# RG-LRU gates of a hybrid decoder trunk: one 64-row product per head for both gates, input gates moved between partitions by DMA

## What is computed

```python
def rg_lru(u, w_a, b_a, w_x, b_x, lam):
    ub = u.reshape(bsz, seq, N_RNN_BLOCKS, RNN_BLOCK)          # 16 heads of 64
    r = sigmoid(einsum('bsnc,ncd->bsnd', ub, w_a) + b_a)       # recurrence gate
    i_gate = sigmoid(einsum('bsnc,ncd->bsnd', ub, w_x) + b_x)  # input gate
    log_a = -8.0 * r * softplus(-lam)
    a = exp(log_a)
    beta = sqrt(-expm1(2.0 * log_a))
    b = beta * (i_gate * u)
    # h_t = a_t * h_{t-1} + b_t
```

## Time and profile before

| | us |
|---|---|
| median of 3 runs (1827.29 to 1829.1) | 1828.26 |
| the profiled execution, its own time | 1829.26 |
| its span, first to last instruction | 1827.6 |
| TensorE busy / weight loads | 1784.1 / 1564.4 |
| VectorE busy | 1488.7 |
| ScalarE busy | 1303.0 |
| POOL busy | 107.7 |
| gate products (L1923), 64 records | 15.6 |

### The profile page before, as it was taken

One profiled execution on the slowest core, in us unless ns is written; L12 is line 12 of the kernel. 1 busy time (PEld: TensorE's weight loads), 2 busy tenths in 40 slices (PEclk: granted clock), 3 DMA queues, 4 the chain that ended last, 5 costly groups with the idle time before them and its releaser, 6 DMA issues.

```text
span 1827.6 us, 29753 instructions
## 1 busy us (share of the span) xinstructions
PE 1784.1 (98%) x10521; PEld 1564.4 (86%) x10521; DVE 1488.7 (81%) x1948; ACT 1303.0 (71%) x1726; POOL 107.7 (6%) x138
## 2 busy tenths in 40 slices
PE   6999999999999999999999999999999999999997
PEld 6998999999879999978888888888888888888785
DVE  7888667666468886669989989989899898998996
ACT  6756547454477657567888888788888888888786
POOL 1200000000010200012000000010000000000300
PEclk8999999999999999999999999999999999999999
DMA  9663565565545744667999999999999999999991
GB/s 308 205 191 117 177 201 187 185 200 201 192 153 174 221 149 141 202 190 260 395 384 387 375 380 387 370 388 382 369 388 374 382 383 374 383 376 382 393 363 48
DMA packets 276048, 517.01 MB, mean 283 GB/s; under 512 B 10754, under 2 KB 114052, under 8 KB 275972
## 3 DMA queue, kind: packets, MB, share of 16 engines
q1 hardware_dynamic: 268400, 493.81, 76.3%
q0 software_dynamic: 7248, 22.06, 3.7%
q10 hardware_dynamic: 324, 0.12, 0.0%
HBM read 503.87 MB, written 7.88 MB: 280 GB/s over the span
## 4 chain that ended last, share of the span: by engine, by line
PE 84%; DVE 8%; ACT 6%; issue 2%; DMA 1%; DVEq 0%; SPq 0%; ACTq 0%
PE bank L1768 79%; DVE wlo L1115 3%; ACT whi L656 1%; PE bank L2225 1%; DMA raw<-in_moe_w_gate_dram 1%; ACT SC L832 1%; PE bank L1923 1%; ACT SQJ L667 1%; DVE RIN L1222 1%; DVE SC L1250 1%; ACT SC L827 0%; PE bank L1879 0%; ACT HH L714 0%; PE bank L2235 0%; DVE HL L1133 0%
## 5 line engine op out<-in xcount | busy, mean ns | idle before, releaser
L1115 DVE TENSOR_TENSOR wlo<-raw,whi 128x1024 fp32r<-128x1024 f32 x880 | 1030.1, 1221 | 154.8 <-ACT whi L656 151.8
L656 ACT ACTIVATE whi<-raw 128x1024 fp32r<-128x1024 f32 x880 | 919.9, 1059 | 308.7 <-PE bank L1768 300.9
L1768 PE MATMUL bank<-HH,whi 128*128 128x256 f32 x1296 | 364.0, 281 | 0.0
L1768 PE MATMUL bank<-HL,whi 128*128 128x256 f32 x1296 | 360.1, 278 | 0.0
L1768 PE MATMUL bank<-HH,wlo 128*128 128x256 f32 x1296 | 360.1, 278 | 0.0
L1768 PE MATMUL bank<-whi,XGH 128*128 128x512 f32 x896 | 355.0, 396 | 1.8 <-DVE wlo L1115 1.6
L1768 PE MATMUL bank<-whi,XGL 128*128 128x512 f32 x896 | 350.4, 391 | 0.0
L1768 PE MATMUL bank<-wlo,XGH 128*128 128x512 f32 x896 | 349.4, 390 | 0.0
L1768 PEld LDWEIGHTS bank<-HH,whi 128*128 128x128 f32 x1296 | 243.8, 188 | 0.9 <-issue 0.7
L1768 PEld LDWEIGHTS bank<-HH,wlo 128*128 128x128 f32 x1296 | 244.5, 189 | 0.0
L1768 PEld LDWEIGHTS bank<-HL,whi 128*128 128x128 f32 x1296 | 243.8, 188 | 0.2
(11 more groups left out here) (349 smaller groups left out, 2073.0 us busy)
## 6 DMA issues: line engine op xcount, KB each, us to landing
raw<-in_moe_w_gate_dram SPq DMA_DIRECT2D x112, 1024.0 KB, 7.2
raw<-in_moe_w_up_dram SPq DMA_DIRECT2D x112, 1024.0 KB, 7.7
raw<-in_moe_w_down_dram SPq DMA_DIRECT2D x112, 1024.0 KB, 6.0
raw<-in_w_in_dram SPq DMA_DIRECT2D x56, 1024.0 KB, 6.0
raw<-in_ffn_w_gate_dram SPq DMA_DIRECT2D x14, 1024.0 KB, 5.0
raw<-in_ffn_w_up_dram SPq DMA_DIRECT2D x14, 1024.0 KB, 5.0
raw<-in_ffn_w_down_dram SPq DMA_DIRECT2D x14, 1024.0 KB, 5.0
raw<-in_w_proj_a_dram SPq DMA_DIRECT2D x8, 1024.0 KB, 5.3
```

Source lines behind the costliest of these rows:

```text
L656: nc.scalar.activation(whi[b % SPL][:, r], raw[b % RAW][:, r], ACT.Copy).then_inc(s_hi, 1)
L1115: v.tensor_tensor(wlo[b % SPL][:, r], raw[b % RAW][:, r], whi[b % SPL][:, r].bitcast(F32), ALU.subtract).then_inc(s_lo, 1)
L1768: ins = mm(dst, a, b, start=start and n == 0, stop=stop and n == 2, skip_group_check=True)
```

## The change

- BD becomes half as large: for tile t, rows of head h hold both its matrices side by side, the recurrence gate's in columns 64h to 64h+63 and the input gate's in the other 64. No zeros are needed, and both memsets go.
- A gate product is one product of 64 rows per head: the head's 64 rows of BD and of U. Its 128 output rows are the head's recurrence gates on the head's own partitions and its input gates on the other half. The two heads go to two banks, (3, 7) or (5, 6).
- So Sigmoid of head 0 goes to T2 and that of head 1 to IG: each of the two tiles holds recurrence gates on one half of the partitions and input gates on the other. Tanh and Exp need the recurrence gates alone, so each is issued twice, over 64 partitions. The wait (`link`) moves behind the second Sigmoid.
- The input gates go to their own partitions in a new tile IX by DMA, issued by POOL within `exchange`, two transfers of 64 partitions for each pair of tiles (`input_halves`), when ScalarE has written the pair (`s_gx`). `input_gates` multiplies IX by U and waits for all 8 transfers of the layer (`s_ix`), as do the decays.
- IX lies where V goes, so the copies of V wait for `recurrence_input`.
- The two biases are loaded in four pieces in the order of the new output rows; 9 loads in place of 7.

```diff
         o_bd = o_rin + 8 * KB + LANE
-        BD = at("BD", o_bd, [P, 2, KT, P])
+        BD = at("BD", o_bd, [P, KT, P])
...
         V = at("V", o_q + 16 * KB, [P, BLK, D])
+        IX = at("IX", o_q + 16 * KB, [P, KT, SEQ])
...
+        LRU_BANK = ((3, 7), (5, 6))
...
-                        pool.dma_start(BD[HD * h:HD * h + HD, kind, :, HD * h:HD * h + HD], pairs[h]).then_inc(s_bd, 16)
-
-            pool.wait_ge(s_bdz, 1)
+                        d = HD * (kind ^ h)
+                        pool.dma_start(BD[HD * h:HD * h + HD, :, d:d + HD], pairs[h]).then_inc(s_bd, 16)
...
+            def input_halves(layer, j):
+
+                pool.wait_ge(s_gx, 4 * layer + j + 1)
+                two = slice(2 * j, 2 * j + 2)
+                pool.dma_start(IX[0:HD, two, :], T2[HD:P, two, :]).then_inc(s_ix, 16)
+                pool.dma_start(IX[HD:P, two, :], IG[0:HD, two, :]).then_inc(s_ix, 16)
+
             def exchange(layer):
 
+                input_halves(layer, 0)
+                input_halves(layer, 1)
                 for i in range(8):
                     n = 8 * layer + i
+                    if i in (1, 2):
+                        input_halves(layer, i + 1)
                     pool.wait_ge(s_eva, eva(layer, 4 + i))
...
                     act.wait_ge(s_gt, KT * layer + t + 1)
-                    bank = B[3 if t % 2 == 0 else 7]
                     col = layer * KT + t
-                    link(nc.scalar.activation(T2[:, t, :], bank[:, 0:SEQ], ACT.Sigmoid, bias=V2[:, 80 + col:81 + col]))
-                    nc.scalar.activation(IG[:, t, :], bank[:, SEQ:], ACT.Sigmoid, bias=V2[:, 96 + col:97 + col])
+                    for h, dst in enumerate((T2, IG)):
+                        c = 96 + 16 * h + col
+                        ins = nc.scalar.activation(dst[:, t, :], B[LRU_BANK[t % 2][h]][:, 0:SEQ], ACT.Sigmoid,
+                                                   bias=V2[:, c:c + 1])
+                    link(ins)
+                    if t % 2:
+                        act.sem_inc(s_gx, 1)
                     if layer == 0 and t == 0:
                         act.wait_ge(s_c2, 1)
-                    nc.scalar.activation(TH[:, t, :], T2[:, t, :], ACT.Tanh,
-                                         scale=SPLAM[:, col:col + 1]).then_inc(s_ga, 1)
+                    for h, src in enumerate((T2, IG)):
+                        r = slice(HD * h, HD * h + HD)
+                        ins = nc.scalar.activation(TH[r, t, :], src[r, t, :], ACT.Tanh, scale=SPLAM[r, col:col + 1])
+                    ins.then_inc(s_ga, 1)
 
             def decays(layer, g):
 
+                act.wait_ge(s_ix, 128 * (layer + 1))
                 for t in range(4 * g, 4 * g + 4):
                     col = layer * KT + t
-                    ins = nc.scalar.activation(T2[:, t, :], T2[:, t, :], ACT.Exp, scale=SPNEG[:, col:col + 1])
+                    for h, src in enumerate((T2, IG)):
+                        r = slice(HD * h, HD * h + HD)
+                        ins = nc.scalar.activation(T2[r, t, :], src[r, t, :], ACT.Exp, scale=SPNEG[r, col:col + 1])
                 ins.then_inc(s_al, 1)
...
                             act.wait_ge(s_rc, 6 * layer + 2)
+                        act.wait_ge(s_bl, KT * layer + c - 7)
...
             def input_gates(layer):
-                dve.wait_ge(s_ga, KT * (layer + 1))
-                v.tensor_tensor(IG[:, :, :], IG[:, :, :], U[:, :, :], ALU.mult).then_inc(s_iu, 1)
+                dve.wait_ge(s_ix, 128 * (layer + 1))
+                v.tensor_tensor(IX[:, :, :], IX[:, :, :], U[:, :, :], ALU.mult).then_inc(s_iu, 1)
...
-                v.tensor_tensor(IG[:, i, :], IG[:, i, :], SQ[:, i, :], ALU.mult).then_inc(s_bl, 1)
+                v.tensor_tensor(IG[:, i, :], IX[:, i, :], SQ[:, i, :], ALU.mult).then_inc(s_bl, 1)
...
-                bank = B[3 if t % 2 == 0 else 7]
-                for kind in range(2):
-                    ins = mm(bank[:, SEQ * kind:SEQ * kind + SEQ], BD[:, kind, t, :], U[:, t, :],
-                             start=True, stop=True)
+                if n == 1:
+                    pe.wait_ge(s_tc, 4)
+                for h in range(2):
+                    r = slice(HD * h, HD * h + HD)
+                    ins = mm(B[LRU_BANK[t % 2][h]][:, 0:SEQ], BD[r, t, :], U[r, t, :], start=True, stop=True)
                 ins.then_inc(s_gt, 1)
```

More of the change, by code:

```diff
@@ L51 @@
 GROUP = (1, 2, 3, 4, 0, 5, 6)
-N_LD0, N_LD1, N_LD2 = 2, 7, 3
+N_LD0, N_LD1, N_LD2 = 2, 9, 3
 TURN_X = (31, 34)
@@ L278, in bass_hybrid_rglru_diffattn_moe @@
         s_iu = sem("s_iu")
+        s_gx = sem("s_gx")
+        s_ix = sem("s_ix")
         s_bl = sem("s_bl")
@@ L508, in _ @@
             pool.memset(JC[:, :, EXPERTS:], 0.0).then_inc(s_pool, 1)
-            pool.memset(BD[:, :, :, :], 0.0).then_inc(s_bdz, 1)
             pool.iota(IOTA[:, :], [[1, P]], base=0, channel_multiplier=0,
@@ L559, in _ @@
             pool.wait_ge(s_pe, 2 * (GATE0 + 2))
-            pool.memset(BD[:, :, :, :], 0.0).then_inc(s_bdz, 1)
             pool.memset(RIN[:, :, 0:3], 0.0).then_inc(s_bdz, 1)
-            pool.wait_ge(s_bdz, 3)
             gates(1)
@@ L643, in _ @@
             for v in (conv_w.rearrange("l j (t p) -> (l j t) p", p=P), conv_b.rearrange("l (t p) -> (l t) p", p=P),
-                      lru_ba.rearrange("l (t p) -> (l t) p", p=P), lru_bx.rearrange("l (t p) -> (l t) p", p=P),
                       lru_lam.rearrange("l (t p) -> (l t) p", p=P)):
@@ L648, in _ @@
                 at_row += n
+            for kind, v in enumerate((lru_ba, lru_bx)):
+                v = v.rearrange("l (t p) -> (l t) p", p=P)
+                for h in range(2):
+                    row, d = 96 + 16 * h, HD * (kind ^ h)
+                    load(R2[row:row + 16, d:d + HD], v[:, HD * h:HD * h + HD], s_ld1)
             def hi(b, jobs=0):
@@ L1185, in convolve @@
                 if j == 0:
-                    dve.wait_ge(s_bdz if layer else s_pool, 3 if layer else 12)
+                    dve.wait_ge(s_bdz if layer else s_pool, 1 if layer else 12)
                 for tap in range(4):
@@ L1425, in _ @@
             dve.wait_ge(s_ld2, 16 * N_LD2)
-            lam = V2[:, 112:128]
+            lam = V2[:, 80:96]
             v.scalar_tensor_tensor(out=SM[:, 16:32], in0=lam, scalar=-1.0, in1=lam, op0=ALU.mult, op1=ALU.min)
```

## The result

| | before | after |
|---|---|---|
| median, us (4 runs each) | 1828.68 | 1858.07 |
| ratio, 95% interval | | 1.0155 (1.0143 to 1.0166) |
| span of the profiled execution | 1827.6 | 1855.5 |

The change makes the kernel 1.55% slower. The forecast was slower, by 18.5 us; it is 29.4, and 1858 lies above the range of 1837 to 1852.

The account below looks back on a forecast made before the run. It took the mutual waits of ScalarE and VectorE from chunk 14, not the 98% busy TensorE, as the bound. 1829.26 + 9.8 (layer 0) + 8.7 (layer 1) = 1847.8, or 1846.8 us against the median; range 1837 to 1852.

Parts of the forecast that it names:

- The ring's terms: ScalarE and VectorE waiting on each other from chunk 14: V's copies add 1.55 us in chunk 14, 3.15 in chunk 15.
- The waits' whole price of 5.95: V's copies waiting for recurrence input, transfers landing early: 1.25 in chunk 12, 1.55 in 14, 3.15 in 15, each layer.
- The entrance: Layer 0, from the late input gates to the first mask: that mask comes 5.1 us late.
- the half activations: ScalarE's Tanh and Exp over 64 partitions: 0.405 us each, bounds 0.2 and 0.5; a tile's turn 1.67 for 1.28.
- They land in 5.9: Input-gate transfers land 5.9 us after issue, bounds 1.9 and 9.9; in layer 0 at 72.3 us, 6.55 late.
- At no cost: At the start, BD's dropped memset (1.8 us on POOL) and two extra loads cost nothing; without the loads' cover, 0.9.
- That cancels: Layer 0: the gate group of chunk 3 comes some 0.5 us later, cancelling chunk 4's saving; chunk 5 ends unchanged.
- 8.7 forecast: Loss in layer 1: 8.7 us against 9.8 in layer 0, since it is 1.1 less late at the start.
- TensorE idles some 4 us at 114, behind the ring's back: Head 0's scores wait for rotation 7, so TensorE idles some 4 us at 114, behind the ScalarE and VectorE waits.
- slower by less: Rival: transfers land in 2 us, V's waits stay at 5.95 a layer, 2.3 saved in layer 1; 1837.9 us, chance 0.18.
- the quiet exchange: Earlier q/k transfers with no weights in flight: 64 KB landed in 1.9 to 2.4 us, cited for the early-landing rival.
- halves do not overlap: Rival: TensorE's gate products run one by one, 0.3 us more a group; 1847 to 1848 us, chance 0.04.

Follow-up runs that it names:

- clock_kept: The changed kernel plus 34 unused TensorE products ahead of the wait for head 0's scores, filling TensorE's idle time; 1862.35 us.
- clock_kept_16: The changed kernel plus 16 unused TensorE products ahead of the wait for head 0's scores; 1856.75 us.
- gates_held: The changed kernel, but POOL sends layer 0's gate matrices only when the first chunk of weights has landed; 1858.90 us.

## Why the prediction was wrong

The sign, the places and the order of the mechanism held. Where it failed, by its own steps, in layer 0:

- **The ring's terms were right.** From the first mask to exp 0 I had +1.55, from there to exp 1 the rest of 3.15: the lags of mask, exp 0 and exp 1 are 9.8, 11.3 and 14.4, steps of 1.5 and 3.1. The waits' whole price of 5.95 was measured twice in layer 0, at 6.1 and 6.3 (in layer 1 at 7.2 and 5.9).
- **The entrance was mis-sized**: lag of the first mask 9.8 where I had 5.1. Of the 4.7, **the half activations** are the largest term. "I price one like a full one, 0.405": it is 0.52, so an Exp group grows by 2.55 and not 1.62, twice, and a tile's turn is 1.91 and not 1.67: 2.1 in all. The 0.52 is just above the upper of my bounds (0.5), and I had not carried even that into the range. (Measured from `hi` to `hi`, 7.96 for 5.45 and 6.56 for 4.22, the two stretches grew by 2.5 and 2.3, 0.2 less in sum.)
- **"They land in 5.9"**: 7.0 in layer 0, 8.1 in layer 1, both inside the bound of 9.9: 1.1 and 2.2 us.
- **"At no cost"**: the dropped memset cost 0.9 in this execution (first RIN at 31.97 for 31.11; 0.9 to 2.2 in the eight kernels here that send the gate matrices at 3.9). I looked at who waits for POOL and not at what POOL's transfers collide with when they start 1.8 us earlier.
- **"That cancels"**, of chunk 3's stall: behind that group chunk products went on at 50.43 for 48.41, which is 1.2 us lost beyond the late start, and the group of chunk 4 gives back 0.5. Tile 6 came at 64.56 for 63.08, 0.6 later than by the start alone.
- 2.1 + 1.1 + 0.9 + 0.6 = 4.7, the entrance's whole error. All four went the same way, and my range had allowed for half of what one of them could add. The whole of it in both layers, 8.0, would still have given only 1854.8.
- **Layer 1**: 8.7 forecast, 13.0 measured, by the same two prices (1.9 for Exp, 2.2 for the landing).
- "TensorE idles some 4 us at 114, behind the ring's back": it idles 7.6 us, and clock_kept and clock_kept_16 show that it is behind.
- The rival "slower by less" rested on landings near 2 us. The first two pairs of a layer do land in 2.3 to 6.5 us in after, but the last transfer of a layer, the one that is waited for, took 4.8 at the least in any kernel here (gates_held, layer 0). The row that it rested on in the earlier trace rows has three of the quiet exchange's four transfers; the fourth landed in 3.7. The rival "halves do not overlap" fell by 1.49 us a group, where I had 1.40 to 1.41.

## What to carry to other kernels

Products saved on an engine that is busy 98% of the time were worth at most 1.5 us a layer in any kernel here, because the chain is elsewhere just behind them; what they asked of the other engines made a layer 13 us longer. Price a split instruction at its full recorded duration, as the halves here turned out, not at the distance of whole ones. And look for the split that leaves the data where most of its readers want it: four quarter products gave the same TensorE time as two halves and left ScalarE as it was.

## What the runs showed that I had not expected

- Activations over 64 partitions, in turn on the lower and the upper half, start 0.52 us apart, each 0.51 long; whole ones start 0.405 apart with 0.50. The Trainium skill, "ScalarE: Activation LUTs", What ACT_TABLE_LOAD costs, says that activations back to back overlap by some 93 ns. Whole ones agree with it (0.50 - 0.405 = 0.095), 64-partition ones here do not overlap at all. Whether successive ones on the same half would was not tried.
- Four products of 64x64, each reading one half of the rows and writing one half of the partitions in two banks, run at once: 16 records in 1.09 us, where eight of 64x128 take 1.14.
- The granted clock fell to its lower level 2.0 us into TensorE's idle time of 7.6 and stayed there for 10.2 us, nearly five of them with products running again; with 7.1 us of unused products in that gap it did not fall there.
- Where 0.52 MB of gate matrices were sent at 3.9 us, `hi` of chunk 0 came 0.8 to 1.6 us later than in before (eight kernels); where at 5.6, as in before, by nothing or 0.2 later (three); where at 11.5 or 11.6, on time, but `hi` of chunk 2 4.3 and 4.8 us later (two). The middle one was the kernel's by the length of a memset.
